# First attention and retention: scores and values in two stacked passes, first pair staged during the value rows

## The chip, the cores and the metric

The kernel runs on 1 core of one Trainium2 chip as one program written by hand for five engines: TensorE (matmuls), VectorE, ScalarE, GpSimd and SyncE, which issues the transfers. The metric is the device time of the core in microseconds (us). The engines meet through named counting semaphores: an instruction adds to one when it is done, another waits until the count is reached.

## The reference

Two transformer blocks on 512 tokens of width 1024, in float32. What matters here are two pieces, each with 8 heads of width 64:

```
# first block: stick-breaking attention
z = (q / 8) . k                                   # scores, per head
log_keep = where(s < t, log_sigmoid(-z), 0)
log_after = cumsum(log_keep, reversed) - log_keep
a = where(s < t, exp(log_sigmoid(z) + log_after), 0)
o = a . v
# second block: retention
scores = (rope(q) . rope(k)) * 64**-0.5 * gamma_h ** (t - s)   # for s <= t
o = scores . v                                     # then a group norm, times silu(gate)
```

log_sigmoid(-z) is minus softplus(z) = -log(1 + exp(z)), which is what the kernel calculates.

## The kernel before

**High and low parts.** Every float32 operand of a matmul is split into two parts of TensorE's faster type fp32r: ScalarE writes the high part (a copy that rounds), VectorE the low part (the full value less the high one). A product is then three passes into the same PSUM bank: high x high, high x low, low x high. Weights come in groups of 256 columns (1 MB) through two raw buffers: SyncE loads, ScalarE makes w_hi (1.9 us), VectorE w_lo (2.3 us), TensorE multiplies. A weight load waits until the low part of the group two before is made.

**The stages around the change.** In the first block the input is multiplied with the glu weights, then `qk` (4 groups, result qkT: four chunks of queries and four of keys, two heads of 64 rows in a chunk of 128 partitions), `val` (2 groups, value rows) and `gate` (8 groups). The gate matmuls are laid between the steps of the attention, one group to a head. In the second block the same is done with `ret_qk`, `ret_val` and then `latent` and `ret_gate` (2 groups each, one tile of 24 matmuls to a head). Meanwhile VectorE works through the taps of a convolution (`conv_beside`, `some_taps`; two taps of 0.75 us at a time) and columns of the modulation (`ada_column`).

**A pair of heads.** Before a pair starts, `stage_qk` on ScalarE and VectorE writes the parts of its queries (scaled by 1/8) and its keys. A chunk of keys holds both heads, so the queries of each head sit in a buffer of their own whose other 64 rows are zero (`clear_other_heads`, once for each stage): the contraction over 128 rows then gives one head. `stage_v` writes the high and low parts of the pair's values; the values product gives 128 rows of which the head's 64 are kept.

**A head of the attention** (`head` on TensorE L581, ScalarE L979, VectorE L1546):
1. TensorE: `scores`, four blocks of keys against the queries behind them (512, 384, 256 and 128 columns), three passes each, and a mask matmul. Into z, 1280 columns in two halves of 512 and 768.
2. VectorE: z clamped at 40 (L1554); ScalarE: exp, log(1 + x) (L985, L988); VectorE: the maximum with z (L1558); ScalarE and VectorE: high and low part (t_hi, t_lo). Beside it TensorE does 32 gate matmuls of 0.23 us each.
3. TensorE: running sums (L595, L598) from t_hi and t_lo into z; then 16 gate matmuls. Meanwhile ScalarE: exp of z, high part; VectorE: low part.
4. TensorE: `values` (L542), three passes; ScalarE moves the head's 64 rows of o_ps into qkT (L1006), behind a one-element write `apart`.

**A head of the retention**: scores; VectorE multiplies z with the decay (L1782), high and low part; TensorE has a tile of 24 matmuls beside it; values; ScalarE moves the result (L1222). From head 4 on pieces of the group norm and of the latent norm lie between (`beside_scores`, `beside_values`, `after_gate`); head 3 has the rotated key of the later attention (`key_rope`).

Each engine runs its list in order. `run` lays the step of one weight group (`ahead`) at a fixed place of each evacuation. The first pair is staged where one stage ends: on ScalarE behind the last value rows (L1008 to L1011; L1229 to L1236 in the retention), on VectorE behind the last modulation column (L1570, L1571; L1855 to L1857).

## Time and profile before

| | |
|---|---|
| median of 3 runs | 1462.67 us (1461.22 to 1462.8) |
| profiled execution: its time, its span | 1461.86 us, 1460.1 us |
| mean granted clock of TensorE | 0.979 |
| busy: TensorE, VectorE, ScalarE, GpSimd | 95%, 60%, 43%, 6% of the span |
| first attention with its gate groups | 143 to 292 us of the span |
| retention with latent and gate groups | 875 to 961 us |

A row of a timeline has the start, the duration, the engine, the line, the operation and what it writes and reads; in square brackets stands how long the engine was idle before it, and who released it. Rows of several instructions are merged (x8). TensorE overlaps a matmul with the next, so a row's duration is about 0.17 us longer than the distance to the next one's start. PEclk is the clock that TensorE was granted, as a share of 2.4 GHz.

### The profile page before, as it was taken

To read this page: it belongs to the slowest core of one execution; us is meant where nothing else is said; L and a number is where in the kernel's file an instruction comes from. 1 tells how busy PE (TensorE), PEld (TensorE's weight loads), DVE (VectorE), ACT (ScalarE), POOL (GpSimd) and SP (SyncE) were. 2 spreads that over 40 slices of the span, in tenths; PEclk is the share of its full clock that TensorE was granted. 3 is DMA by queue.
4 is the path that set the end of the run, shared out by engine and by line. 5 is a ranking of instruction groups with operands and counts; after the bars stand their busy time and mean duration, and the time that the engine had idled before them with its cause. 6 is when DMAs were issued, how large, how long until landed. Compare 5 with 4: busy or idle time off the path is not lost. (4 is left out here: it accounts for less than half of the span.)

```text
span 1460.1 us, 16589 instructions
## 1 busy us (share of the span) xinstructions
PE 1380.1 (95%) x6344; PEld 1134.4 (78%) x6344; DVE 872.8 (60%) x1057; ACT 629.3 (43%) x767; POOL 90.8 (6%) x67
## 2 busy tenths in 40 slices
PE   6998999979979999999997989988999999999997
PEld 3788888857748888888885788778778888888885
DVE  4799888768674432332335646777556754773663
ACT  4322666574354222221324744567645522432332
POOL 0000000010300093000001000000020000000001
PEclk9999999999989999999998999999999999999999
DMA  9532111035624423223231221040122232223212
GB/s 372 195 130 87 58 57 43 29 120 186 257 80 139 163 87 112 90 89 113 79 101 58 87 87 58 15 108 1 58 90 102 96 109 93 86 86 115 87 66 78
DMA packets 27110, 148.56 MB, mean 102 GB/s; under 512 B 3184, under 2 KB 3696, under 8 KB 14512
## 3 DMA queue, kind: packets, MB, share of 16 engines
q1 hardware_dynamic: 27056, 147.83, 28.2%
q8 instruction: 35, 0.57, 0.2%
q14 instruction: 19, 0.16, 0.0%
HBM read 143.88 MB, written 2.10 MB: 100 GB/s over the span
## 5 line engine op out<-in xcount | busy, mean ns | idle before, releaser
L1370 DVE TENSOR_TENSOR w_lo<-raw,w_hi 128x2048 fp32r<-128x2048 f32 (+2 forms) x114 | 251.5, 2206 | 122.4 <-ACT w_hi L838 118.9
L838 ACT ACTIVATE w_hi<-raw 128x2048 fp32r<-128x2048 f32 (+2 forms) x109 | 196.6, 1804 | 108.6 <-PE psum L482 80.6
L482 PE MATMUL psum<-h_hi,w_hi 128*128 128x512 f32 x712 | 180.0, 393 | 2.4 <-DVE w_lo L1370 2.4
L482 PE MATMUL psum<-h_hi,w_lo 128*128 128x512 f32 x712 | 178.0, 390 | 0.0
L482 PE MATMUL psum<-h_lo,w_hi 128*128 128x512 f32 x712 | 177.3, 389 | 0.0
L482 PEld LDWEIGHTS psum<-h_hi,w_hi 128*128 128x128 f32 x712 | 133.1, 189 | 31.0 <-DVE w_lo L1370 3.7
L482 PEld LDWEIGHTS psum<-h_lo,w_hi 128*128 128x128 f32 x712 | 133.6, 188 | 27.8
L482 PEld LDWEIGHTS psum<-h_hi,w_lo 128*128 128x128 f32 x712 | 133.1, 188 | 27.4
L482 PE MATMUL psum<-xg_hi,w_hi 128*128 128x512 f32 x336 | 83.0, 389 | 0.0
L482 PE MATMUL psum<-xg_hi,w_lo 128*128 128x512 f32 x336 | 83.0, 389 | 0.0
L482 PE MATMUL psum<-xg_lo,w_hi 128*128 128x512 f32 x336 | 83.0, 389 | 0.0
L1670 DVE TENSOR_TENSOR act_p<-act_a,psum 128x512 f32<-128x512 f32 x22 | 15.1, 688 | 112.3 <-PE psum L482 112.3
L482 PE MATMUL psum<-mid_hi,w_hi 128*128 128x512 f32 x312 | 77.7, 389 | 0.1
L482 PE MATMUL psum<-mid_hi,w_lo 128*128 128x512 f32 x312 | 77.6, 389 | 0.0
L482 PE MATMUL psum<-mid_lo,w_hi 128*128 128x512 f32 x312 | 77.5, 389 | 0.0
L482 PEld LDWEIGHTS psum<-xg_hi,w_lo 128*128 128x128 f32 x336 | 63.1, 188 | 13.1
L482 PEld LDWEIGHTS psum<-xg_hi,w_hi 128*128 128x128 f32 x336 | 63.1, 188 | 13.1
L482 PEld LDWEIGHTS psum<-xg_lo,w_hi 128*128 128x128 f32 x336 | 63.1, 188 | 13.1
L1968 DVE TENSOR_TENSOR up_raw<-psum,rs 128x512 f32<-128x512 f32 x44 | 30.3, 688 | 64.2 <-PE psum L482 59.6
L482 PEld LDWEIGHTS psum<-mid_hi,w_hi 128*128 128x128 f32 x312 | 58.5, 188 | 12.6 <-DVE w_lo L1370 0.5
L482 PEld LDWEIGHTS psum<-mid_hi,w_lo 128*128 128x128 f32 x312 | 58.6, 188 | 12.2
L482 PEld LDWEIGHTS psum<-mid_lo,w_hi 128*128 128x128 f32 x312 | 58.6, 188 | 12.2
(341 smaller groups left out, 2247.1 us busy)
## 6 DMA issues: line engine op xcount, KB each, us to landing
raw<-w_ffn_in SPq DMA_DIRECT2D x22, 1024.0 KB, 4.8
raw<-w_up SPq DMA_DIRECT2D x22, 1024.0 KB, 4.7
ada_first<-ada SPq DMA_DIRECT2D x16, 512.0 KB, 11.3
raw<-w_gate SPq DMA_DIRECT2D x8, 1024.0 KB, 4.7
raw<-w_mix_out SPq DMA_DIRECT2D x8, 1024.0 KB, 4.8
raw<-w_ffn_out SPq DMA_DIRECT2D x8, 1024.0 KB, 4.8
raw<-w_down SPq DMA_DIRECT2D x8, 1024.0 KB, 4.8
ada_mid<-ada SPq DMA_DIRECT2D x11, 512.0 KB, 6.0
```

The source lines that it names most:

```text
L482: last = mm(ps, w[slot][:, k, t * P:(t + 1) * P], part(xv, k0 + k), start=first, stop=final)
L838: A(w_hi[slot][:, 0:stage.kc, :], raw[slot][:, 0:stage.kc, :], ACT.Copy).then_inc(sem["w_hi_done"], 1)
L1370: return tt(out_lo, full, high.bitcast(F32), ALU.subtract)
L1670: free(stage, k, lambda: tt(act_p[s][:, :], act_a[s][:, :], bank[2 * s + 1], ALU.mult))
L1968: by_rs = lambda: tt(up_raw[t][s][:, :], bank[2 * s + t], rs[:, :], ALU.mult)
```

## The change

**Scores in two passes.** The zero rows of the query buffers get content: in `q_both` the head's own 64 rows hold the high part of its queries, the other 64 rows the low part. The keys then have to stand in both halves: `key_hi[s]` and `key_lo[s]` hold head s's keys twice. One pass with key_hi and one with key_lo give (high + low) x (high + low). **Values in two passes.** The weights for a head are 128 columns, 64 of high and 64 of low values (`att_v`, `ret_v`); the product gives 64 rows of each, which ScalarE copies (rows 0 to 63) and VectorE adds (rows 64 to 127, `add_low_part`, `join_head`). A product low x low is added that was not there before.

**Copies of the keys.** Transfers within SBUF bring the first head's keys into both halves of `key_dup` (2 x 512 KB) and, when they have landed, the second head's keys over the first's in qkT (512 KB). SyncE issues them in its list, before and between the loads of the first two groups of `gate` or `latent`. The same is done in the retention with rqk and `rkey_dup`.

**First pair.** `stage_qk(0)` moves to the second group of the value stage, on ScalarE in front of its evacuation and on VectorE behind the first group's modulation columns (in the retention behind the second group's weights, with two decays). The clears are gone. A pair's staging now has two full keys to split instead of one. `stage_v` moves on ScalarE to the end of the pair before.

**Softplus.** max(z, log(1 + exp(min(z, 40)))) becomes max(z, 0) + log(1 + exp(-|z|)): the clamp on VectorE goes, ScalarE takes the absolute value from PSUM, and the maximum and the addition are one VectorE instruction. The running sums of the first key block and the first block of the values now wait for the first half of t_lo alone.

The core of the difference (the declarations of buffers, the retention's twins of edits that are shown for the attention, and moved lines are left out):

```diff
@@ SyncE
+            def duplicate_first(keys, dup, done):
+                for s in range(2):
+                    sp.dma_start(dup[head_rows(s), :, :], keys[0:HD, PAIRS:, :]).then_inc(sem[done], 16)
+            def duplicate_second(keys, done):
+                sp.wait_ge(sem[done], 32)
+                sp.dma_start(keys[0:HD, PAIRS:, :], keys[HD:P, PAIRS:, :]).then_inc(sem[done], 16)
+            stage_loads(st["val"])
+            sp.wait_ge(sem["group_free"], st["val"].g0)
+            duplicate_first(qkT, key_dup, "key_dup")
+            load(st["gate"], 0, 0)
+            duplicate_second(qkT, "key_dup")
+            load(st["gate"], 1, 1)
...
+            sp.wait_ge(sem["rp_done"], 2 * PAIRS)
+            duplicate_first(rqk, rkey_dup, "rkey_dup")
+            load(st["latent"], 0, 0)
+            duplicate_second(rqk, "rkey_dup")
+            load(st["latent"], 1, 1)
@@ TensorE
-                    for n, (kk, qq) in enumerate(((key_hi, q_hi), (key_hi, q_lo), (key_lo, q_hi))):
-                        last = mm(z[:, a:a + w], kk[:, kb * P:(kb + 1) * P], qq[s][:, kb * P:S],
+                    for n, kk in enumerate((key_hi, key_lo)):
+                        last = mm(z[:, a:a + w], kk[s][:, kb * P:(kb + 1) * P], q_both[s][:, kb * P:S],
...
-                    for n, (vv, aa) in enumerate(((vs_hi, p_hi), (vs_hi, p_lo), (vs_lo, p_hi))):
-                        last = mm(o[:, kb * P:S], vv[:, v_at, kb * P:(kb + 1) * P], aa[:, a:a + w],
+                    if second and kb == 1:
+                        pe.wait_ge(sem[second[0]], second[1])
+                    for n, aa in enumerate((p_hi, p_lo)):
+                        last = mm(o[:, kb * P:S], v[:, s, kb, :], aa[:, a:a + w],
...
+                pe.wait_ge(sem["spl_done"], 2 * n + 1)
+                for part in (t_hi, t_lo):
+                    mm(z[:, 0:S], tri_r, part[:, 0:S], start=False, stop=True, skip_group_check=True)
                 pe.wait_ge(sem["spl_done"], 2 * n + 2)
...
-                pe.wait_ge(sem["al_done"], 2 * n + 2)
+                pe.wait_ge(sem["al_done"], 2 * n + 1)
+                values(o_ps, att_v, s, t_hi, t_lo, ("al_done", 2 * n + 2)).then_inc(sem["o_done"], 1)
@@ ScalarE
+            def stage_qk(i, q, dup):
+                for s in range(2):
+                    A(q_both[s][head_rows(s), :], chunk(q, i, head_rows(s)), ACT.Copy, scale=HD ** -0.5).then_inc(sem["qk_hi"], 1)
+                A(key_hi[0][:, :], chunk(dup, i), ACT.Copy).then_inc(sem["qk_hi"], 1)
+                A(key_hi[1][:, :], chunk(q, PAIRS + i), ACT.Copy).then_inc(sem["qk_hi"], 1)
+            def val_rows(i, s, k, ahead):
+                if k == 1:
+                    act.wait_ge(sem["key_dup"], 48)
+                    stage_qk(0, qkT, key_dup)
+                rows_of(st["val"], v_rows)(i, s, k, ahead)
...
+                for j, (a, b) in enumerate(HALVES):
+                    act.wait_ge(sem["z_done"], n + 1)
+                    A(zbuf[:, a:b], z[:, a:b], ACT.Abs).then_inc(sem["zm_done"], 1)
                 for j, (a, b) in enumerate(HALVES):
                     act.wait_ge(sem["zm_done"], 2 * n + j + 1)
-                    A(zbuf[:, a:b], zbuf[:, a:b], ACT.Exp).then_inc(sem["e_done"], 1)
+                    A(zbuf[:, a:b], zbuf[:, a:b], ACT.Exp, scale=-1.0).then_inc(sem["e_done"], 1)
...
-                apart(0)
-                A(chunk(qkT, i, rows), o_ps[rows, :], ACT.Copy).then_inc(sem["o_evac"], 1)
+                A(chunk(qkT, i, head_rows(s)), o_ps[0:HD, :], ACT.Copy).then_inc(sem["o_half"], 1)
+                if s and not final:
+                    stage_v(i + 1, v_rows, att_v)
@@ VectorE
-                for a, b in HALVES:
-                    ts(zbuf[:, a:b], z[:, a:b], 40.0, None, ALU.min).then_inc(sem["zm_done"], 1)
...
-                    tt(zbuf[:, a:b], z[:, a:b], zbuf[:, a:b], ALU.max).then_inc(sem["sp_done"], 1)
+                    stt(zbuf[:, a:b], z[:, a:b], 0.0, zbuf[:, a:b], ALU.max, ALU.add).then_inc(sem["sp_done"], 1)
...
                 some_taps(2, 3)
-            clear_other_heads()
-            stage_qk(0, 0, qkT, qkT)
+                dve.wait_ge(sem["o_half"], n + 1)
+                add_low_part(chunk(qkT, i, head_rows(s))).then_inc(sem["o_evac"], 1)
...
+            def join_head(n):
+                dve.wait_ge(sem["ro_half"], n + 1)
+                add_low_part(rqk[head_rows(n % 2), n // 2, :]).then_inc(sem["ro_evac"], 1)
```

What stood on ScalarE from the end of the first value group to the attention's first head; the `pair` buffers are the high parts of queries and keys, raw_52 and raw_53 the two weight buffers:

```order
L838 ACTIVATE w_hi_54<-raw_52 128x2048 [waits tile_done,raw_full0]
L961 ACTIVATE v_rows<-psum 128x2x256 [waits tile_done]
L963 ACTIVATE v_rows<-psum 128x2x256 [waits group_free,tile_done]
L1008 ACT_TABLE_LOAD
L973 ACTIVATE pair_78<-qkT 64x512 [waits ada_sum,group_free]
L973 ACTIVATE pair_79<-qkT 64x512
L974 ACTIVATE pair_82<-qkT 128x512
L861 UNCONDITIONAL_BRANCH
L861 ISA
L977 ACTIVATE att_v_hi<-v_rows 128x512
```

The same place in the changed kernel:

```order
L987 ACTIVATE v_rows<-psum 128x2x256 [waits group_free,tile_done]
L993 ACTIVATE pair_77<-qkT 64x512 [waits key_dup]
L993 ACTIVATE pair_78<-qkT 64x512
L994 ACTIVATE pair_79<-key_dup 128x512
L995 ACTIVATE pair_80<-qkT 128x512
L862 ACTIVATE w_hi_54<-raw_52 128x2048 [waits tile_done,raw_full0]
L985 ACTIVATE v_rows<-psum 128x2x256 [waits tile_done]
L987 ACTIVATE v_rows<-psum 128x2x256 [waits group_free,tile_done]
L998 ACTIVATE att_v<-v_rows 128x4x2x64 [waits ada_sum,group_free]
```

The staging of queries and keys, now four instructions with a wait for the copies, has moved ahead of the gate weights and of the second group's value rows; behind the rows only the values remain.

VectorE at the end of an odd head with a next pair, before; qkT is where a head's output goes, conv_77 and conv_tmp are the taps' sums:

```order
L1501 SCALAR_TENSOR_TENSOR conv_tmp<-u,vec,conv_tmp 128x512
L1500 REGISTER_ALU
L1501 ISA [waits tap]
L1501 SCALAR_TENSOR_TENSOR conv_77<-u,vec,conv_77 128x512
L1399 REGISTER_ALU
L1399 COMPARE_AND_BRANCH
L1370 TENSOR_TENSOR att_v_lo<-v_rows,att_v_hi 128x512 [waits v_hi]
L1554 TENSOR_SCALAR zbuf<-psum 128x512 [waits z_done]
L1554 TENSOR_SCALAR zbuf<-psum 128x768
L1501 SCALAR_TENSOR_TENSOR conv_tmp<-u,vec,conv_tmp 128x512 [waits tap]
L1501 SCALAR_TENSOR_TENSOR conv_77<-u,vec,conv_77 128x512 [waits tap]
L1558 TENSOR_TENSOR zbuf<-psum,zbuf 128x512 [waits l_done]
```

The same place in the change (conv_76 is the sum that was conv_77):

```order
L1556 SCALAR_TENSOR_TENSOR conv_76<-u,vec,conv_76 128x512
L1604 REGISTER_ALU
L1538 ISA [waits o_half]
L1538 TENSOR_TENSOR qkT<-psum,qkT 64x512
L1435 REGISTER_ALU
L1435 COMPARE_AND_BRANCH
L1406 TENSOR_TENSOR att_v<-v_rows,att_v 128x4x2x64 [waits v_hi]
L1556 SCALAR_TENSOR_TENSOR conv_tmp<-u,vec,conv_tmp 128x512 [waits tap]
L1556 SCALAR_TENSOR_TENSOR conv_76<-u,vec,conv_76 128x512 [waits tap]
L1593 SCALAR_TENSOR_TENSOR zbuf<-psum,zbuf 128x512 [waits l_done]
L1593 SCALAR_TENSOR_TENSOR zbuf<-psum,zbuf 128x768 [waits l_done]
L1406 TENSOR_TENSOR t_lo<-zbuf,t_hi 128x512 [waits sph_done]
```

A wait for ScalarE's copy and the join stand between the last tap and the next pair's values, and the two clamps are gone.

SyncE between the loads of the value weights and the loop over the gate groups, in the change (before, the loop over all gate groups followed at once):

```order
L326 DMA raw_52<-w_val 128x2048 [waits w_lo_done]
L326 DMA raw_53<-w_val 128x2048 [waits w_lo_done]
L330 REGISTER_ALU
L330 COMPARE_AND_BRANCH
L378 DMA key_dup<-qkT 64x2048 [waits group_free]
L378 DMA key_dup<-qkT 64x2048
L326 DMA raw_52<-w_gate 128x2048 [waits w_lo_done]
L383 DMA qkT<-qkT 64x2048 [waits key_dup]
L326 DMA raw_53<-w_gate 128x2048 [waits w_lo_done]
```

The three copies stand in the list with their waits, so the first two gate groups are loaded behind and between them.

## Rows read from the trace of the kernel before

**Rows 1.** Timeline of TensorE at the attention's first scores: start us, us, engine, line, operation, idle before.

```profile
143.07 1.62 PE L531 MATMUL psum<-pair,pair 128*128 128x512 f32 x3 [5.18 <-DVE pair L1370]
...
147.48 2.62 PE L482 MATMUL psum<-h_hi,w_hi 128*128 128x512 f32 x8
```

**Rows 2.** Timeline of TensorE at the retention's first two heads.

```profile
875.04 3.76 PE L531 MATMUL psum<-pair,pair 128*128 128x512 f32 x12 [5.23 <-DVE pair L1370]
...
878.59 2.35 PE L482 MATMUL psum<-h_hi,w_hi 128*128 128x512 f32 x8
...
886.27 2.08 PE L531 MATMUL psum<-pair,pair 128*128 128x512 f32 x12
...
888.19 2.04 PE L482 MATMUL psum<-h_hi,w_hi 128*128 128x512 f32 x8
```

**Rows 3.** Busy us (x instructions) by stretch: PE, PEld, DVE, ACT, POOL, PEclk, DMA share, GB/s.

```profile
140.00:145.00 5.00, 1.93 (x5) 1.68 (x6) 4.22 (x8) 2.25 (x4) 0.00 (x0) 0.69 0.01 3
...
870.00:880.00 10.00, 4.96 (x17) 4.48 (x18) 3.16 (x6) 6.82 (x11) 0.00 (x0) 0.66 0.00 0
...
964.00:970.00 6.00, 4.15 (x17) 2.69 (x15) 4.45 (x7) 3.10 (x6) 0.00 (x0) 1.00 0.99 203
```

**Rows 4.** Timeline of TensorE, end of head 1 to the gate matmuls of head 3.

```profile
178.24 1.97 PE L482 MATMUL psum<-h_lo,w_hi 128*128 128x512 f32 x8
...
180.40 0.50 PE L542 MATMUL psum<-t_hi,att_v_hi 128*128 128x512 f32 x1 [0.19 <-DVE t_lo L1370]
...
182.38 0.90 PE L531 MATMUL psum<-pair,pair 128*128 128x512 f32 x3
...
184.75 2.06 PE L482 MATMUL psum<-h_hi,w_hi 128*128 128x512 f32 x8
...
203.00 2.06 PE L482 MATMUL psum<-h_hi,w_hi 128*128 128x512 f32 x8
```

**Rows 5.** Timeline of TensorE, retention heads 4, 6 and the queries behind them.

```profile
922.73 1.95 PE L654 MATMUL psum<-rope_t,ones 128*128 128x512 f32 x4 [1.03 <-ACT rope_t L1174]
...
948.02 1.10 PE L646 MATMUL psum<-rope_t,block_mean 128*128 128x512 f32 x2 [1.02 <-ACT rope_t L1161]
...
968.49 1.10 PE L646 MATMUL psum<-sq_up,block_mean 128*128 128x512 f32 x2 [1.85 <-ACT sq_up L1161]
```

**Rows 6.** Timeline of VectorE before the attention's first head.

```profile
138.27 0.08 DVE L1442 DVE_READ_ACCUMULATOR2_ANT mod<- 128x1 f32 x1
...
140.87 1.34 DVE L1537 SCALAR_TENSOR_TENSOR pair<-qkT,pair 64x512 fp32r<-64x512 f32 x2
```

**Rows 7.** Timelines of ScalarE and VectorE, attention head 1.

```profile
168.84 1.35 ACT L988 ACTIVATE zbuf<-zbuf 128x512 f32<-128x512 f32 x2
...
175.71 0.63 ACT L974 ACTIVATE pair<-qkT 128x512 fp32r x1
...
176.55 1.30 ACT L998 ACTIVATE zbuf<-psum 128x512 f32<-128x512 f32 x2 [0.21 <-PE psum L595]
...
166.50 1.55 DVE L1554 TENSOR_SCALAR zbuf<-psum 128x512 f32<-128x512 f32 x2 [2.01 <-PE psum L534]
...
172.10 0.96 DVE L1370 TENSOR_TENSOR t_lo<-zbuf,t_hi 128x768 fp32r<-128x768 f32 x1 [0.32 <-ACT t_hi L991]
...
178.19 0.69 DVE L1370 TENSOR_TENSOR pair<-qkT,pair 128x512 fp32r<-128x512 f32 x1
```

**Rows 8.** Timeline of VectorE, retention head 3 to 4.

```profile
914.32 0.69 DVE L1751 TENSOR_TENSOR rope_t<-psum,sin_mla 64x512 f32<-64x512 f32 x1
...
916.48 1.68 DVE L1782 TENSOR_TENSOR rp<-psum,decay 128x512 f32<-128x512 f32 x4
```

**Rows 9.** Timelines of VectorE and TensorE at the attention's end.

```profile
292.08 0.75 DVE L1501 SCALAR_TENSOR_TENSOR conv<-u,vec,conv 128x512 f32<-128x512 f32 x1
...
293.34 1.96 PE L616 MATMUL psum<-u,ones 128*128 128x512 f32 x4 [0.99 <-ACT qkT L1006]
```

**Rows 10.** Timeline of VectorE, last rotated key of the retention.

```profile
850.69 0.69 DVE L1737 TENSOR_TENSOR rqk<-rope_t,swapped 128x512 f32<-128x512 f32 x1
```

More of the change, by code:

```diff
@@ L325, in load, with stage_loads @@
                              dram["w_" + stage.name][bass.ds(k, 1)].rearrange("g p n -> p (g n)")).then_inc(raw_full[slot], 16)
-            def stage_loads(stage):
-                with sp.Fori(0, stage.n // 2) as i:
+            def stage_loads(stage, begin=0):
+                with sp.Fori(begin, stage.n // 2) as i:
                     for s in range(2):
@@ L372, in _ @@
                 load(st["qk"], k, k - 2)
[L373 to L374 removed]
+            def duplicate_first(keys, dup, done):
[10 more added lines that the diff above has]
+            load(st["gate"], 1, 1)
+            stage_loads(st["gate"], 1)
+            stage_loads(st["att_out"])
             sp.wait_ge(sem["o_evac"], HEADS)
@@ L594, in head @@
                     for part in (t_hi, t_lo):
-                        last = mm(z[:, a:a + w], tri_r, part[:, a:a + w], start=False, stop=True, skip_group_check=True)
+                        if kb:
+                            last = mm(z[:, a:a + w], tri_r, part[:, a:a + w], start=False, stop=True, skip_group_check=True)
                         for later in range(kb + 1, QB):
@@ L993, in head @@
                 A(chunk(gates, 2 * n), bank[2 * s], ACT.Copy)
-                if not ahead() and s:
-                    stage_qk(i + 1, qkT, qkT)
+                final = ahead()
+                if s and not final:
+                    stage_qk(i + 1, qkT, key_dup)
                 for j, (a, b) in enumerate(HALVES):
@@ L1122, in _, with decays @@
             run(st["ret_qk"], rotary)
+            def decays(n):
+                A(decay[n % 4][:, :], lag[:, :], ACT.Exp, scale=scol("log_gamma", n)).then_inc(sem["dec_done"], 1)
             def values_by_rs(i, s, k, ahead):
                 ahead()
+                if k == 1:
+                    act.wait_ge(sem["rkey_dup"], 48)
+                    stage_qk(0, rqk, rkey_dup)
+                    act.wait_ge(sem["in_lag"], 16)
+                    for n in range(2):
+                        decays(n)
                 if k == 0:
@@ L1483, in _, with stage_qk, stage_v, add_low_part @@
                 free(st["glu"], k, lambda: tt(u[:, k, PAD:PAD + S], glu_sig[k % 2][:, :], bank[2 * k], ALU.mult))
+            def stage_qk(i, staged, q, dup):
+                for s in range(2):
+                    dve.wait_ge(sem["qk_hi"], 4 * staged + 4 * i + s + 1)
+                    stt(q_both[s][head_rows(1 - s), :], chunk(q, i, head_rows(s)), HD ** -0.5, q_both[s][head_rows(s), :].bitcast(F32),
+                        ALU.mult, ALU.subtract).then_inc(sem["qk_lo"], 1)
+                for s, full in enumerate((chunk(dup, i), chunk(q, PAIRS + i))):
+                    dve.wait_ge(sem["qk_hi"], 4 * staged + 4 * i + 3 + s)
+                    less(key_lo[s][:, :], full, key_hi[s][:, :]).then_inc(sem["qk_lo"], 1)
+            def stage_v(i, staged, v, both):
+                dve.wait_ge(sem["v_hi"], staged + i + 1)
+                part_of = lambda k: both[:, :, :, HD * k:HD * k + HD].rearrange("p s b d -> p b s d")
+                less(part_of(1), v[:, :, bass.ds(P * i, P)].rearrange("p b (s d) -> p b s d", s=2), part_of(0)).then_inc(sem["v_lo"], 1)
+            def add_low_part(dst):
+                return tt(dst, o_ps[HD:P, :], dst, ALU.add)
             sums = [conv_tmp, conv3]
@@ L1518, in evac @@
                             ada_column(val_bufs[r], ADA_FIRST + r)
+                        if step == 4:
+                            stage_qk(0, 0, qkT, key_dup)
                 return evac
```

119 lines of the change are left out of this document (46 added, 73 removed).

## The prediction

> **What bounds the kernel now.** I read the page first: TensorE is busy 95% of the span (the table above), so a change pays where it removes work from TensorE or a wait in front of it. Then I read TensorE's timeline over the two stages that the change touches: the first attention (143 to 292 us) and the retention (875 to 961 us). The reader is to see three things. First, both stages begin with a hole: TensorE idles 5.18 us [rows 1] and 5.23 us [rows 2] until VectorE has written the low parts of the first pair, and both are followed by matmuls at the lower clock (mean granted clock 0.69 and 0.66, [rows 3]). Secondly, inside the stages TensorE goes from matmul to matmul: one head of the attention lasts 18.25 us (184.75 to 203.00) or 18.45 us [rows 4], one of the early retention heads 9.28 us, and its idle time there is a few tenths before each values product. Thirdly, from head 4 of the retention on there are waits on ScalarE of about 1 us [rows 5]. So passes taken from TensorE are worth their full time, up to the point where the chains on ScalarE and VectorE end last.
>
> **Passes removed.** Scores and values each drop one of three passes over four blocks of 512, 384, 256 and 128 columns. In the attention the twelve values matmuls run from 180.40 to 182.38, 1.98 us [rows 4]; scores with four mask matmuls take 2.37 us (182.38 to 184.75), of which the masks are some 0.3. In the retention scores take 1.92 us (886.27 to 888.19, [rows 2]). A third of 1.92 is 0.64; I take 0.63 for each pass. 8 heads x 2 passes x 0.63 = 10.1 us in each stage, 20.2 us together. Bounds: 0.57, if all 1280 columns went at the pace of a gate tile's row (8 matmuls of 512 columns in the 1.81 us between such rows), and 0.69, a third of the scores' 2.07 us without masks: 18 to 22 us.
>
> The Trainium skill, "TensorE: Matmul & The Clock Gate", section "Back-to-back issue gap", gives the isolated gap of a matmul at full clock as N/2.4 + 2.5 ns. By that a pass of 1280 columns would be worth 0.54 us and the term 17.4 us. By that rule, the trace does not agree to the tenth: its pass is 0.64 us in the retention's scores.
>
> **First boundary (137.8 us).** Before, TensorE waits 5.2 us, runs the scores in 4.41 us (143.07 to 147.48, [rows 1]) where another head takes 2.37 [rows 4], so 2.04 us more, and the first gate pass in 2.62 where the same row elsewhere reads about 2.0: 0.6 more. That is 7.8 us. Now the staging stands among the value rows. The key copies can be issued when the last query-key tile is evacuated, at 115.5 us. Nearest row for their speed: copies within SBUF move 203 GB/s with the DMA engines 99% busy [rows 3]. 1.05 MB then takes 5.2 us, and with about 1.7 us from issue to first bytes (256 KB landed alone in 3.0 us, less 1.3 us of data) it lands at about 122.5; the gate weights behind it at about 126; the second copy (0.52 MB, 2.6 us) at about 128.5. ScalarE comes to it at 127.0, behind the first group's value rows, and stages until 131; VectorE adds two pieces of 0.67 us and two of 0.69, 2.8 us, and ends its list at 141.1 instead of 138.3 [rows 6]. The four clears and its old staging are gone. TensorE can begin its scores at 137.8 without a wait; margin about 4 us. What is late next is VectorE: conv start, the low values part and two taps bring it to 144.0, while the logarithm of head 0 would be ready at 142.9. The running sums then wait about 0.4 us. Gain 7.4 us.
>
> The Trainium skill, "DMA: Bandwidth & Descriptors", section "Anatomy of one DMA", gives 2.0 us plus bytes at 436 GB/s: the first copies would land in 4.4 us, not 6.9. The rows of this kernel's copies within SBUF show less than half that speed; by the page the margins below would only be wider, the sum the same, and late copies less likely.
>
> **Inside an attention head.** The clamp on VectorE (1.55 us) becomes an absolute value on ScalarE. Nearest row: two halves read from PSUM, 1.30 us; exponentials and logarithms follow at 1.26 to 1.35 us a pair [rows 7]. Scores' end to logarithm: 2.37 us before (166.47 to 168.84), forecast 0.04 + 1.18 + 1.26 = 2.5 us. Bounds: -0.3 us (the clamp's way saved) and +1.5 us (nothing overlaps). VectorE's max-and-add may cost 0.1 us more a head. Low parts were ready at 173.06 [rows 7], TensorE came at 173.63: slack 0.57, and now the first two matmuls (0.45 us) need only the first half. The sums start as before; cost nothing. If that cover went, each further 0.1 us a head would cost 0.8 us in all.
>
> Before the values, even heads wait 0.17 us and odd ones 0.35 (its last gate row starts at 178.24 and needs 1.81; values at 180.40, [rows 4]). With only the first half needed for the first block, the even ones (and head 7) wait no more: -0.17 x 5 = -0.85. Heads 1, 3 and 5 also stage the next pair, and that has grown by one full key: 0.63 us on ScalarE, 0.69 on VectorE [rows 7]. ScalarE's key ended at 176.34, 0.2 us before the sums; now 0.7 us after the exponentials could start. VectorE reaches the low part 0.8 us later, TensorE waits about 0.3 and, at the second block, 0.4: 0.7 for 0.35. +0.35 x 3 = +1.05. Together +0.2 us. The join (64x512 from PSUM, 0.69 us by [rows 8]) waits on VectorE for ScalarE's copy of the upper half; queued behind it are the next low values part and two taps, which end about C + 9.0 us (C the end of the running sums) while the next logarithm comes at C + 9.65: hidden by 0.6 us, by 0.25 in odd heads. At the stage's end it isn't hidden: VectorE has taps until 292.8 [rows 9], then the join, so the mean's first matmul comes 7.0 us after the sums' end where it was 6.76 (293.34). That forfeits head 7's 0.63 + 0.17 and 0.24 more: +1.0 us.
>
> Attention: -10.1 - 7.4 + 0.2 + 1.0 = -16.3 us.
>
> **Retention boundary (869.7 us).** Wait 5.23, scores 3.55 us (875.04 to 878.59) for 1.92, first tile pass 2.35 for 2.04 [rows 2]: 5.2 + 1.6 + 0.3 = 7.1 us. The copies start when the last key is rotated, 851.4 [rows 10]: landed 858.6, latent weights 862 (they were loaded from 842.7; SyncE's order now holds them back 10 us), second copy about 865. ScalarE splits the weights 862 to 864 (before at 859), stages 865 to 867.6, computes two decays, then evacuates; VectorE's last low key is ready at about 868.9. TensorE arrives at 869.65: margin 0.8 us, the thinnest of the change. Gain 7.1, between -0.3 and 7.2 if the copies come up to 8 us later.
>
> **Inside the retention.** Heads 0 to 3: scores' end to low part is about 4.7 us, TensorE's tile 5.5 us, the join lies beside ScalarE's copy of 1.27 us. All passes count. Head 3 to 4: VectorE has the rotated key besides and came to head 4 at 916.48 [rows 8], already 0.1 us late. Now it has 0.69 us more (second key) and the scores end 1.3 us earlier; the squares of head 4 move with VectorE, so the wait at 922.73 [rows 5] grows: values 3 and scores 4 are not gained (1.26) and 0.6 is lost: +1.9. Head 5: ScalarE's further key delays its squares: +0.6. Head 6: ScalarE is the chain from the output of head 5 to 948.02, so scores 6 are not gained: +0.6. Behind head 7 the join, the first query and ScalarE's table load stand in line up to 968.49 [rows 5]; of the last three passes (1.9 us) about 1.1 arrives: +0.8.
>
> Retention: -10.1 - 7.1 + 1.9 + 0.6 + 0.6 + 0.8 = -13.3 us.
>
> **Sum.** The profiled execution took 1461.86 us (span 1460.1), 0.8 below the median of 1462.67, within what the runs differ. 1461.86 - 16.3 - 13.3 = 1432.3. I add 0.7 us for the thin margin at the retention's copies (one chance in ten of 7 us): 1433.0 us.
>
> **Rivals.**
> The chains bind. If ScalarE's three functions in a row, or the join, do not overlap as I read them (upper bound +1.5 us between scores and logarithm), TensorE waits some 0.6 us more in each of 16 heads: +10, 1443 us. For it: slacks of 0.25 to 0.8 us. Against it: every duration is from rows of the same shapes.
> The copies are late. Landing 6 us later costs the retention's whole boundary and about 1 us at the attention's: +8, 1441 us. For it: three transfers in one queue and the weights between them. Against it: the mk copies' measured speed.
> A pass is worth only its columns: the matmul that goes is then one whose weight load and hand-over lay beside others. At the low bound from rows, 0.57, 32 x 0.06 = 1.9 us are missing: 1434.9 us. This is the mechanism behind the Trainium skill's gap above.
> The change doesn't do what it says: the first pair is staged no earlier and the third passes were hidden. 1462 us. Nothing speaks for it, since TensorE has no idle time that would take up the passes.
> Slower: waits before the values grow so long that the clock falls behind each of them, as it did at both boundaries, where it cost 2.6 us (2.04 + 0.6) at 143 us. 16 x (0.7 + 2.6) = 53 us: 1486 us. It decides from the point where 11 of the 16 heads fall (29 / 2.6). Against it: a wait of 1.85 us before 968.49 left the granted clock at 1.00 [rows 3, 5], and the forecast waits are 0.7 us at most in the attention.
>
> **How the numbers follow.** Forecast 0.72 (own range 1428 to 1438), chains 0.10, copies 0.10, the smaller pass 0.05, slower 0.02, nothing 0.01. A measurement of this kernel tells about 0.2% (3 us) from no change. Faster 0.97, same 0.01, slower 0.02. The range runs from 1427.5 (all passes at 0.69 us, -1.9, and 3.6 of the 5.1 us of new waits absent) to 1443, where the chains or late copies would put it.
>
> **What would show each step.** TensorE's wait before the first scores of each stage: under 0.5 us and no lower clock at 140 or 872 us. A head of the attention: 16.9 us (even) and 17.6 us (odd with staging); a retention head 8.0 us up to head 3. Before head 4's squares a wait of near 3 us. The mean's matmul 7.0 us after the sums. If an attention head takes over 18 us, or scores two thirds of which were kept take over 1.9 us, I am wrong on the chain or the pass; if TensorE stands at 870 us for VectorE's low key, the copies were late.

## The result, and the profile after

| | before | after |
|---|---|---|
| median of 4 runs each, us | 1461.95 (1460.01 to 1462.8) | 1444.09 (1442.05 to 1445.13) |
| profiled span, us | 1460.1 | 1443.1 |
| mean granted clock | 0.979 | 0.977 |

Ratio 0.9874, 95% interval 0.9862 to 0.9887: 18.4 us faster (16.5 to 20.2). The forecast was 1433.0 us, in 1427.5 to 1443: the direction held, 11 of the 29 us did not come, and the time lies 1.1 us outside the range.

To find where, take an instruction that both kernels have and subtract its start after from its start before: that is the gain up to there. The first group of rows is TensorE's timeline of the changed kernel through the attention (start us, duration us, engine, line, operation, idle before it and who ended it).

```profile
137.10 0.63 PE L555 MATMUL psum<-pair,pair 128*128 128x512 f32 x2
...
146.85 0.50 PE L618 MATMUL psum<-t_hi,rounded 128*128 128x512 f32 x1 [0.57 <-DVE t_lo L1406]
...
155.40 0.67 PE L555 MATMUL psum<-pair,pair 128*128 128x512 f32 x2
...
172.82 0.68 PE L555 MATMUL psum<-pair,pair 128*128 128x512 f32 x2
...
174.56 2.06 PE L506 MATMUL psum<-h_hi,w_hi 128*128 128x512 f32 x8
...
189.53 0.67 PE L555 MATMUL psum<-pair,pair 128*128 128x512 f32 x2
...
276.79 2.59 PE L645 MATMUL psum<-u,ones 128*128 128x512 f32 x4 [2.19 <-DVE qkT L1538]
```

The wait of 5.18 us ahead of the first scores [rows 1] is gone. Heads take 17.42 us (155.40 to 172.82) and 16.71 (to 189.53) where they took 18.45 and 18.25 [rows 4]; scores with masks take 1.74 us (172.82 to 174.56) for 2.37. The mean's first matmul starts at 276.79, before at 293.34 [rows 9]: gain 16.55 us, forecast 16.3.

Behind it the gain shrinks. The same timeline of the changed kernel, then of the kernel before, at the statistics of the convolution's norm:

```profile
281.60 0.80 PE L519 MATMUL psum<-h_hi,w_hi 128*128 128x512 f32 x1
...
295.92 2.07 PE L467 MATMUL psum<-sq_sum,ones 128*128 128x512 f32 x2 [2.85 <-POOL sq_sum L2060]
297.01 2.69 PE L506 MATMUL psum<-h_hi,w_hi 128*128 128x512 f32 x4
...
302.45 0.84 PE L506 MATMUL psum<-h_hi,w_hi 128*128 128x512 f32 x3
```

```profile
296.45 0.80 PE L495 MATMUL psum<-h_hi,w_hi 128*128 128x512 f32 x1
...
310.79 1.13 PE L443 MATMUL psum<-sq_sum,ones 128*128 128x512 f32 x2 [2.87 <-POOL sq_sum L2015]
311.35 1.50 PE L482 MATMUL psum<-h_hi,w_hi 128*128 128x512 f32 x4
...
314.52 1.07 PE L482 MATMUL psum<-h_hi,w_hi 128*128 128x512 f32 x4
```

The eight matmuls of the mean took 3.11 us before (293.34 to 296.45) and now 4.81 (276.79 to 281.60): gain 14.85. The statistics wait as long as before (2.85 us for 2.87), yet what follows is slower: gain 12.07 at 302.45. Gain 10.9 at the end of retention's value rows (869.65 before, 858.74 after): of the 1.2 us lost on the way, 0.7 stands in TensorE's wait for ScalarE before the next norm's sums of squares (6.71 us for 6.00), 0.3 behind the wait of 3.94 us before the convolution's second stage, which low clock followed before the change too.

The retention in the changed kernel, on TensorE:

```profile
861.07 2.08 PE L555 MATMUL psum<-pair,pair 128*128 128x512 f32 x8 [2.16 <-issue]
862.94 3.05 PE L506 MATMUL psum<-h_hi,w_hi 128*128 128x512 f32 x8
...
870.68 1.43 PE L555 MATMUL psum<-pair,pair 128*128 128x512 f32 x8
871.95 2.06 PE L506 MATMUL psum<-h_hi,w_hi 128*128 128x512 f32 x8
...
879.63 1.46 PE L555 MATMUL psum<-pair,pair 128*128 128x512 f32 x8 [0.79 <-DVE pair L1406]
...
896.61 1.46 PE L555 MATMUL psum<-pair,pair 128*128 128x512 f32 x8 [0.79 <-DVE pair L1406]
...
905.62 3.35 PE L683 MATMUL psum<-rope_t,ones 128*128 128x512 f32 x4 [2.04 <-ACT rope_t L1214]
...
951.00 2.05 PE L675 MATMUL psum<-sq_up,block_mean 128*128 128x512 f32 x2 [2.65 <-ACT sq_up L1201]
```

Against [rows 2]: 2.16 us of the 5.23 are left, with slow matmuls behind. Two new waits of 0.79 us stand ahead of the scores of heads 2 and 4; measured by starts a head with such a wait takes 8.97 us instead of 8.00, so each costs 0.97. Head 4's statistics (`rope_t` x ones, the sums of squares for the latent's norm) wait 2.04 us for 1.03 [rows 5], the last variance 2.65 for 1.85 [rows 5], and the instructions themselves take 3.35 us for 1.95 and 2.05 for 1.10.

Busy time by stretch for those four places, the kernel before ahead of the changed one (columns as in [rows 3]; PEclk is the granted clock):

```profile
293.00:297.00 4.00, 3.66 (x9) 1.77 (x10) 2.50 (x4) 2.39 (x5) 0.00 (x0) 1.00 0.00 0
308.00:315.00 7.00, 4.21 (x17) 3.13 (x18) 3.11 (x3) 5.42 (x6) 2.53 (x2) 1.00 0.86 332
922.00:928.00 6.00, 5.27 (x22) 3.61 (x23) 4.40 (x6) 1.66 (x4) 0.00 (x0) 1.00 0.27 87
968.00:973.00 5.00, 4.51 (x16) 3.10 (x17) 3.57 (x6) 3.33 (x6) 0.00 (x0) 1.00 0.96 238
```

```profile
276.00:282.00 6.00, 5.21 (x9) 2.21 (x10) 3.14 (x5) 2.19 (x4) 0.00 (x0) 0.72 0.00 0
295.00:302.00 7.00, 6.08 (x13) 4.14 (x14) 1.95 (x1) 3.56 (x4) 0.87 (x1) 0.51 0.64 239
905.00:911.00 6.00, 5.38 (x12) 2.76 (x13) 2.99 (x4) 1.00 (x2) 0.00 (x0) 0.72 0.30 90
950.00:955.00 5.00, 4.00 (x8) 2.10 (x9) 2.85 (x5) 3.40 (x6) 0.00 (x0) 0.66 0.97 247
```

Four places that ran at full clock before do not now; behind the attention's first scores the low clock of [rows 3] is gone (1.00 from 137 to 142 us). The mean over the run barely moved, so it hides this.

Why the first scores of retention are late stands on the timelines of the DMA queue, ScalarE and VectorE in the changed kernel:

```profile
840.50 1.13 SPq L378 DMA_DIRECT2D rkey_dup<-rqk  x2
841.68 2.03 SPq L326 DMA_DIRECT2D raw<-w_latent  x1
847.50 0.46 SPq L383 DMA_DIRECT2D rqk<-rqk  x1
848.00 0.58 SPq L326 DMA_DIRECT2D raw<-w_latent  x1
...
853.97 1.92 ACT L862 ACTIVATE w_hi<-raw 128x2048 fp32r<-128x2048 f32 x1 [5.70 <-DMA raw<-w_latent]
857.34 1.28 ACT L993 ACTIVATE pair<-rqk 64x512 fp32r<-64x512 f32 x2 [1.45 <-DMA rqk<-rqk]
...
855.91 2.29 DVE L1406 TENSOR_TENSOR w_lo<-raw,w_hi 128x2048 fp32r<-128x2048 f32 x1 [12.64 <-ACT w_hi L862]
858.24 1.41 DVE L1525 SCALAR_TENSOR_TENSOR pair<-rqk,pair 64x512 fp32r<-64x512 f32 x2
...
860.28 0.68 DVE L1406 TENSOR_TENSOR pair<-rqk,pair 128x512 fp32r<-128x512 f32 x1
```

Two transfers that the staging needs are late. The first latent weights (1 MB, issued at 841.68) land at 853.96, the second copy (512 KB, issued at 847.50) at 857.33, 9.8 us after its issue; half a microsecond behind it another 1 MB of weights was put into the same queue. TensorE was there at 858.91. What it waits for is VectorE's last low key, ready at 860.96, and VectorE works without a gap from 855.91 on: the low part of the first latent weights, then the staging. So the weights' landing sets the wait. The second copy follows closely: ScalarE has the second key's high part at 859.8, so without the late weights VectorE's last low key would come at about 860.5 (an estimate: 859.8 and the 0.7 us of its row), half a microsecond earlier.

Theory from here: the passes and the early staging gave what was forecast, and the missing 11 us are (a) transfers sharing the queue at retention's start, (b) VectorE's staging ending behind the values, (c) lower clock behind short waits. Rival: the passes are worth less than 0.63 us since the chains bind.

### The profile page after: what moved, and what is told of

It is laid out like the page before. It is cut to its first block and busy times, and to the rows that moved or that the text cites. A ratio compares the mean times of both kernels' runs of the same rounds, so it can differ in the third digit from the quotient of the medians.

```text
span 1443.1 us, 16364 instructions
## 1 busy us (share of the span) xinstructions
PE 1364.2 (95%) x6216; PEld 1115.5 (77%) x6216; DVE 872.9 (60%) x1057; ACT 638.8 (44%) x782; POOL 90.5 (6%) x67
## 5 line engine op out<-in xcount | busy, mean ns | idle before, releaser
L1705 DVE TENSOR_TENSOR act_p<-act_a,psum 128x512 f32<-128x512 f32 x22 | 15.1, 687 | 112.4 <-PE psum L506 112.4
L506 PEld LDWEIGHTS psum<-mid_hi,w_hi 128*128 128x128 f32 x312 | 58.5, 188 | 12.6 <-DVE w_lo L1406 0.5
```

Of the source, the lines that this page charges most:

```text
L506: last = mm(ps, w[slot][:, k, t * P:(t + 1) * P], part(xv, k0 + k), start=first, stop=final)
L1705: free(stage, k, lambda: tt(act_p[s][:, :], act_a[s][:, :], bank[2 * s + 1], ALU.mult))
```

## The experiments

Each stands against runs of the kernel before on the same chip (medians 1461.9 to 1462.8).

**Third pass put back.**

```
-for n, kk in enumerate((key_hi, key_lo)):
+for n, kk in enumerate((key_hi, key_lo, key_lo)):
-for n, aa in enumerate((p_hi, p_lo)):
+for n, aa in enumerate((p_hi, p_lo, p_lo)):
```

> The changed kernel with one more pass in the scores and in the values of every head of both stages (the low part is multiplied twice, so the numbers differ in the last digits; it stands for the third pass of before). Theory: a pass is worth 0.63 us on the path in each of 16 heads, 32 of them 20.2 us; in retention they fill the two waits of 0.79 us at the pair boundaries (-1.6), so 1444.1 + 18.6 = about 1463, heads of the attention 17.4/18.1 us. Rival one, the chains over ScalarE and VectorE bind in the heads and the missing 11 us were never in the passes: under +12 us, 1456 or less. Rival two, a pass is worth only its columns at 0.445 ns (0.57): +16.6, 1461.

Measured 1456.69 us, ratio 0.9966 [0.9952, 0.9979]: +12.6. The theory's 18.6 missed; the total fits the first rival. Its rows don't:

```profile
158.38 0.91 PE L555 MATMUL psum<-pair,pair 128*128 128x512 f32 x3
...
194.82 0.91 PE L555 MATMUL psum<-pair,pair 128*128 128x512 f32 x3
...
879.69 2.08 PE L555 MATMUL psum<-pair,pair 128*128 128x512 f32 x12
...
889.29 2.11 PE L555 MATMUL psum<-pair,pair 128*128 128x512 f32 x12 [0.16 <-DVE pair L1406]
...
917.22 1.95 PE L683 MATMUL psum<-rope_t,ones 128*128 128x512 f32 x4 [1.41 <-ACT rope_t L1214]
```

Two heads of the attention take 36.44 us (158.38 to 194.82) for 34.13: 0.58 us a pass. Scores of retention grow by 0.65 us. But the waits of 0.79 shrink to 0.16, 2.04 to 1.41, 2.65 to 1.84, and the statistics run in 1.95 us, at full clock. From the first scores of retention to the last variance the kernel is 4.7 us longer (94.6 for 89.9) where eight heads have 10.1 us of matmuls more. So the passes are worth their size while they stand in a row, and the chains at the ends of stages, with the clock, take back over a third (7.6 of 20.2). My expectation had counted only two of those waits.

**Late staging.**

```
-act.wait_ge(sem["key_dup"], 48); stage_qk(0, qkT, key_dup)     # in val_rows
+act.wait_ge(sem["key_dup"], 48); stage_qk(0, qkT, key_dup)     # ahead of run(gate)
... the same on VectorE, and both for rqk behind ret_val
```

> The changed kernel with the staging of the first pair of both stages behind the value rows again, everything else kept. Theory: the attention's boundary is worth what its rows gave (7.4) and retention's only about 3 to 4, since its second copy came late and the clock fell there: +10 to +12 us, 1455. Rival, both boundaries are worth their forecast and the loss lies all elsewhere: +14.5, 1458.6. Rival, early staging hinders later work: +8 or less, 1452.

Measured 1452.30 us, 0.9938 [0.992, 0.9957]: +8.2, below the theory, at the second rival. By rows the second head of the attention starts 6.2 us later (161.60 for 155.40) and retention loses 2.6 more. But the low clock behind the convolution's statistics is absent here (their two matmuls take 1.13 us, not 2.07), which gives 2.8 us back; without that the edit would cost 11.0, in the theory's range, so the second rival isn't shown.

**Fillers.** Matmuls into a bank that nobody reads, at four waits.

```
+fill(bank[4], h_hi[:, 0, :], 8)    # ahead of the mean
+fill(bank[4], h_hi[:, 4, :], 10)   # ahead of stat_sum("conv_ln")
+fill(o_ps, h_hi[:, 0, :], 7)       # ahead of head 4's statistics
+fill(bank[4], lat_hi[:, 0, :], 9)  # ahead of group_var(.., 2, ..)
```

> The changed kernel with matmuls that nobody reads put into four waits of TensorE: 8 of 128x512 before the mean (wait 2.19), 10 before the statistics of the convolution's norm (2.85), 7 before head 4's squares (2.04), 9 before the variance beside the up-projections (2.65). They add work and take no wait's end away. Theory (the clock falls behind these waits, and that is where some of the missing time went): no granted clock under 1.00 behind those places, the matmuls behind them at full rate, -1.7 -2.5 -1.7 -1.0 = -6.9 us, 1437 (1436 to 1440 where a filler ends late). Rival (the low clock costs nothing since other engines end last, or the clock falls at the next wait instead): 1443 to 1446.

Measured 1442.86 us, 0.9875 [0.9854, 0.9896]: 1.2 us less than the changed kernel, within what medians differ, so the time does not decide. Its stretches do:

```profile
279.00:284.00 5.00, 4.71 (x14) 2.34 (x13) 3.01 (x6) 2.84 (x6) 0.00 (x0) 1.00 0.00 0
296.00:303.00 7.00, 6.38 (x27) 4.62 (x26) 2.84 (x2) 3.73 (x4) 1.07 (x1) 1.00 0.71 261
903.00:909.00 6.00, 5.64 (x25) 3.74 (x24) 4.55 (x6) 2.34 (x5) 0.00 (x0) 1.00 0.27 87
947.00:952.00 5.00, 4.61 (x17) 3.17 (x18) 3.56 (x7) 3.21 (x6) 0.00 (x0) 1.00 0.93 256
```

At all four the clock stays at 1.00, with waits of 0.29 to 0.62 us left. From the mean to the first matmul of the mix (`mix_out`, the stage that joins the outputs) it takes 58.77 us for 63.34 (-4.6, forecast -4.2), from retention's first scores to the last variance 88.07 for 89.93 (-1.9), and behind the variance 1.4 less. Two things took 5.7 of these 7.8 us back: the last attention (+2.9; the granted clock was 0.74 from 1008 to 1021 us, where the changed kernel had 0.86 from 1011 to 1023, so the rival's "at the next wait" is right in part), and a first head that waited 2.21 us for VectorE where the profiled run of the changed kernel waited 0.57. The second copy of keys was late again:

```profile
133.20 1.28 ACT L1002 ACTIVATE pair<-qkT 64x512 fp32r<-64x512 f32 x2 [5.83 <-DMA qkT<-qkT]
...
149.69 0.50 PE L623 MATMUL psum<-t_hi,rounded 128*128 128x512 f32 x1 [2.21 <-DVE t_lo L1415]
```

ScalarE stages at 133.20 instead of 129.21, VectorE's columns and taps queue behind, TensorE waits inside head 0, and the mean starts 2.9 us later. The same stands in the third-pass run (1.95 us). So the attention's copies were at the edge too, which one trace had hidden.

**Staging by head.** Query and key of head 0, then of head 1, on ScalarE and VectorE (not shown) and in TensorE's wait.

```
-                if s == 0:
-                    pe.wait_ge(sem["qk_lo"], 4 * i + 4)
+                pe.wait_ge(sem["qk_lo"], 4 * i + 2 * s + 2)
```

> The changed kernel with a pair staged head by head (query and key of head 0, then of head 1) on ScalarE and VectorE, and the scores of a head waiting for its own half alone; the first head of a stage so waits for the first two copies of keys only. Theory (VectorE's 2.7 us of staging ends 0.8 us behind the values): the waits of 0.79 us before the scores of heads 2 and 4 of retention go, and the wait of 2.16 us at its start falls to 0.9 or less with its low clock: -1.6 -1.3 to -2.8 = -2.9 to -4.4, 1440 to 1441. Rival (these waits are cover for the chain behind them, which then waits as much in the head's values): 1443 to 1444.

Measured 1441.87 us, 0.9861 [0.9836, 0.9885]: -2.2, a little short, and the interval overlaps the changed kernel's, so the rows have to decide. Heads 1 to 4 of retention start 8.00 us apart (871.62, 879.62, 887.62, 895.62), the forecast's 8.0, so the waits of 0.79 us (0.97 by starts) were VectorE's staging. But head 4's statistics then wait 3.13 us for 2.04, which takes 1.1 of 1.9 back: the rival is right in that part. In the attention the edit costs: the mean starts at 279.57 for 276.79. That the time fell even so is clock, 1.00 here behind the mean and behind head 4's statistics (1.7 us each), which the edit does not explain.

Retention's first wait stayed (2.06), although head 0 no longer needs the second copy. VectorE shows why:

```profile
858.20 2.29 DVE L1405 TENSOR_TENSOR w_lo<-raw,w_hi 128x2048 fp32r<-128x2048 f32 x1 [13.86 <-ACT w_hi L860]
...
861.24 0.69 DVE L1405 TENSOR_TENSOR pair<-rkey_dup,pair 128x512 fp32r<-128x512 f32 x1
```

Head 0's two low parts again stand directly behind the low part of the first latent weights, whose load landed at 856.2, and TensorE starts at 862.03. This run takes the second copy out of the wait and leaves the wait: the late weights are enough for it.

**Loads apart.**

```
+load(st["latent"], 0, 0)
 sp.wait_ge(sem["rp_done"], 2 * PAIRS)
 duplicate_first(rqk, rkey_dup, "rkey_dup")
-load(st["latent"], 0, 0)
 duplicate_second(rqk, "rkey_dup")
+sp.wait_ge(sem["rkey_dup"], 48)
 load(st["latent"], 1, 1)
... the same for qkT, key_dup and the gate's weights
```

> The changed kernel with the 1 MB weight load that stood between the key copies issued ahead of them and the next one held until the second copy has landed, in both stages. Theory (the second copy shares the queue with that load: 9.8 us for 0.5 MB in retention, 7.3 to 10.3 in the attention): it lands in 4.5 to 5.5 us, the wait of 2.16 us at retention's start and the low clock behind it go, -3.5; in the attention the staging on ScalarE comes before 129 in every run and the first head's wait stays at 0.6, -0 to -1.5: 1439.5 to 1441. Rival (the boundary in retention is set by the high parts of the weights and the value rows' copies, not by the key copies): wait of 1.5 us or more stays, 1443 to 1444.

Measured 1435.61 us, 0.9812 [0.9799, 0.9825]: -8.5, twice what was expected, with nothing but the order and the waits of SyncE's transfers changed.

```profile
834.81 1.13 SPq L378 DMA_DIRECT2D rkey_dup<-rqk  x2
841.66 0.46 SPq L383 DMA_DIRECT2D rqk<-rqk  x1
845.76 0.34 SPq L326 DMA_DIRECT2D raw<-w_latent  x1
...
853.05 1.39 PE L557 MATMUL psum<-pair,pair 128*128 128x512 f32 x8
854.27 2.06 PE L508 MATMUL psum<-h_hi,w_hi 128*128 128x512 f32 x8
856.17 1.98 PE L508 MATMUL psum<-h_hi,w_lo 128*128 128x512 f32 x8
```

The second copy lands 4.1 us after its issue (9.8 before the edit). The first latent weights, issued at 826.13, are there long before ScalarE takes them at 842.46, and VectorE's last low key is ready at 849.5. TensorE's first scores of retention wait for nothing, and the tiles behind them run at full rate. The edit does two things, the load ahead of the copies and the next one held back, and no run separates them. From the value rows' end to the second tile pass the gain over the kernel before grows by 8.0 us (16.6 to 24.6), 7.4 without the head's own pass: forecast 7.1. The stretches behind the mean and behind the convolution's statistics are at 1.00 as well, although their waits are unchanged (2.19 and 2.85 us): 3.2 us of the gain up to the mix (3.9 us) is clock that this edit does not explain, and 1.8 us more come between the mix and the end of retention's value rows, where nothing was edited.

**Squares first.**

```
+if n == 4:
+    latent_squares()
 act.wait_ge(sem["rp_f"], n + 1)
```

> The changed kernel with ScalarE's two squares of the latent done before head 4's high part instead of behind it, the weights' high part and a copy. Theory: the wait of 2.04 us before head 4's statistics goes and the low clock behind it, -2.0 -1.4 = -3.4 us, 1440.7; what stays is the wait for the head's low part, some 0.3. Rival (the head's own chain over rp and its parts ends as late): 1443.5.

Measured 1445.88 us, 0.9879 [0.9864, 0.9894]: no gain. Up to the third square's sum 3.0 us were gained (19.52 us from head 4's scores for 22.56) and 2.7 lost behind it; and the first head waited 2.23 us for the late copy.

**Mean and statistics moved.**

```
-pe.wait_ge(sem["o_evac"], HEADS); mm(o_ps, ones, ...)
+mm(bank[4], ones, ...)
-stat_sum("conv_ln")              # ahead of weight group 2
+... stat_sum("conv_ln")          # behind it
```

> The changed kernel with two edits at the end of the attention: the mean's matmuls go into bank 4 and so no longer wait for the last head's output to be joined, and the sum of the convolution's squares stands one weight group (5.4 us) later. Theory: the waits of 2.19 and 2.85 us and the low clock behind both go or fall under 1 us: -1.3 -1.7 and -2.8 -2.5, less 1 for what comes late behind = -7, 1437. Rival (the chain over POOL, ScalarE and VectorE to the convolution's second stage sets the end, so that the wait of 3.94 us before it grows by as much): 1441 to 1444.

Measured 1438.77 us, 0.9838 [0.9824, 0.9851]: -5.3. The mean waits 1.37 us, now for VectorE's taps; the wait at the statistics is gone, and from the mean to the mix's first matmul it takes 56.88 us for 63.34. The wait ahead of the convolution's second stage grew from 3.94 to 5.18.

**Up-projections first.**

```
-up_query(2); up_query(3); ...; group_var(bank[0], 2, sq_up)
+up_query(2) ... up_query(6);   group_var(bank[0], 2, sq_up)
```

> The changed kernel with three more up-projections (4.1 us) ahead of the group variance that waited 2.65 us for ScalarE's square. Theory: wait and low clock go, -2.6 -1.4 = -4.0, of which the chain over VectorE to the first scores of the last attention (wait 2.12 us now) takes back about half: 1442. Rival one: all is taken back, 1444 to 1445. Rival two: all is kept, 1440.

Measured 1442.38 us, 0.9865 [0.985, 0.9881]: -1.7, the expected 1442, though the runs of the two kernels overlap. By rows the edit is worth 2.6 us: the wait of 2.65 us is 0.32, and from the first up-projection to the last attention's scores it takes 20.28 us for 22.88.

**Loads apart with the third pass.** The first and the fifth edit together.

> The kernel with the loads apart (1435.6) and the third pass of before put back in scores and values, as in the first experiment. There the pass cost 12.6 us net: the rows gave 0.6 us a pass in each head, less waits and low clock that the longer heads covered and a first head that began 2.3 us later. Theory: with the copies apart the same count holds, 20.2 less about 5 us of covered waits and low clock in retention and 1.3 behind the attention = +14, 1449.5. Rival (the first experiment's 12.6 held two effects of the copies that cancelled; without them the passes are worth their full 20.2): 1455.5. Rival: less than 12, 1447 or under.

Measured 1449.51 us, 0.992 [0.9907, 0.9934]: +13.9 over the loads apart, the theory's number. The rival that the copies had hidden the passes' full 20.2 us falls.

**Combinations.** Loads apart, staging by head in retention, the mean and statistics, the up-projections; then with the squares first, or with two fillers (7 ahead of head 4's statistics, 16 ahead of the convolution's second stage).

> All that gained at once: loads apart (-8.5), the pairs of retention staged by head (-1.6 of waits), the mean in bank 4 and the convolution's statistics one weight group later (-5.3, of which some 1.5 was low clock that the loads alone also spared), the up-projections ahead of the variance (-1.7). Theory (they stand in different places and add): 1444.1 - 8.5 - 1.6 - 3.8 - 1.7 = 1428.5. Rival (each gain shifts the others' clock and half is given back): 1432 or more.

Measured 1431.51 us, 0.9799 [0.9786, 0.9812]: 3 us short. The loads apart had already spared the clock behind the mean and the statistics: from the mean to the mix the combined kernel takes 57.55 us for their 60.10, 2.5 less where 3.8 were added up. And head 4's statistics now wait 3.14 us.

> The combined kernel with ScalarE's latent squares before head 4's high part as well. Alone that edit gained 3.0 us up to head 5 and gave 2.7 back by the end (wait before the third square's sum 1.94 instead of 1.02, and later ones). Theory: again within 1 us of the combined kernel, 1427.5 to 1429.5. Rival (what gave it back was the up-projections' wait, which is gone now): 3 us less, 1425.5.

Measured 1428.15 us, 0.9772 [0.9759, 0.9785]: 3.4 us less, the rival's size, but the rows don't bear the rival out. Between the two profiled executions (spans 1428.0 and 1424.7 us) 2.3 of the 3.3 us stand ahead of retention's first scores (853.31 and 850.99), where both kernels are the same; from there on the squares are worth 1.0. Head 4's wait is gone, and the next one, before the third square's sum, is 2.47 us with low clock behind.

> The combined kernel with fillers at two waits that remain: 7 matmuls of 128x512 before head 4's statistics (wait 2.04) and 16 before the convolution's second stage (wait 5.2 with the statistics later; 3.6 us of work). Theory (the clock falls behind both): -1.7 behind head 4 and -1.5 to -2 behind the second, 1425 from 1428.5. Rival (the clock falls at the next wait instead or other engines end last): within 1 us of the combined kernel.

Measured 1426.76 us, 0.9757 [0.9741, 0.9773]: 4.8 us less than the combined kernel, with no overlap of their runs, and the fastest of all, 17 us under the changed kernel. The rows give the fillers less than that. From the mean to the mix it takes 55.98 us for 57.55 (-1.6, granted clock 1.00 for 0.62 from 307 to 315 us). From the mix to retention's first scores, where nothing differs, it takes 516.6 for 519.0 (-2.4), and from there to the end 1.2 more. So kernels with work that nobody needs can be faster, and how much of the 4.8 us that work is worth stays open.

## Why the prediction was wrong

- **Passes.** 0.63 us each held in the scores: 2.37 to 1.74 and 1.92 to 1.27 us. Put back, a pass cost 0.58 us in the attention's heads, near the low bound (0.57), and 0.65 in retention's scores. The chains inside the attention's heads did not bind. In all the prediction counted 20.2 us less 5.1 of waits, 15.1; with the loads apart the third pass costs 13.9.
- **First boundary and heads of the attention.** Right: no wait, heads 17.4 and 16.7 us for 17.6 and 16.9, gain 16.55 for 16.3. The margin of "about 4 us" at the copies was not there: ScalarE waited 2.83 us for the second copy and VectorE's last low key was ready at 134.7, 2.4 us before TensorE came, and in five of the other kernels with that order of loads the first head waited 1.95 to 2.25 us.
- **Retention boundary, the step that failed first:** "latent weights 862 ... second copy about 865". I let each transfer run alone behind the one ahead of it, the second copy in 2.6 us. In the queue three of them were under way at once: the second copy was issued while the weights' load was in flight, and the next load 0.5 us behind the copy. Counted from the last rotated key the first latent weights landed 13.5 us later instead of 10.6, the second copy 16.8 instead of 13.6. VectorE's low part of those weights and the staging behind it ended as much later, which turned a margin of 0.8 us into a wait of 2.16 with low clock: 3.4 of 7.1 us gained. With the loads apart it is 7.4. The weights' load ended last and the second copy half a microsecond before it; the run staged by head, which doesn't need that copy for its first scores, waited as long. The rival "the copies are late" named the queue ("the weights between them"), but with a chance of 0.10; the order of the queue was in the code, and the thinnest margin deserved more. The fit cited there from the Trainium skill, "DMA: Bandwidth & Descriptors", is one for transfers that GpSimd issues, and SyncE issues these; no term of the sum rested on it.
- **Retention, heads 0 to 3:** "All passes count" failed by 2 x 0.97 us. The prediction holds the head's low part and the join against TensorE's tile, and says nothing of VectorE's staging of the next pair, for which the next scores wait.
- **Head 4:** the wait is 2.04 us, forecast near 3. Where the two waits ahead of it were taken away it read 3.13, so the step was right and the unforecast waits had made TensorE late. The clock then fell as well.
- **Clock:** forecast at nothing, from a single row at 1.00 behind 1.85 us [rows 5]. Four places fell, at the ends of stages and not in the heads where the "slower" rival looked: from the wait to the first row at full rate 1.7 us behind the mean (4.81 for 3.11 us), 2.8 behind the statistics, 1.7 behind head 4's wait and 1.4 behind the last variance's, 7.6 us. Held at full clock, TensorE took 4.6 and 1.9 us less over the stretches from the mean to the mix and through the retention.
- **The sum:** between the profiled executions 29.6 us were forecast and 17.0 came. Clock 7.6, the boundary 3.7, the staging waits 1.9, 1.2 on the way to retention and 0.3 in heads 5 to 7 make 14.7. Against it stand 0.9 us of waits up to head 4's statistics that were forecast and did not come, 0.3 more gained in the attention and 0.9 behind the last variance, which leaves the 12.6. This is a count of rows, not a proof of each. With the copies apart the same kernel takes 1435.6 us, 2.6 from the forecast, of which some 5 us (3.2 and 1.8 above) is time in places that the edit doesn't touch: luck.

## What to carry to other kernels

A transfer that is waited for shares its queue with all that is under way in it: price them together, issue early what the chain needs first, and hold the next load until it has landed. Then follow the chain back from the instruction that waits; the late transfer that the eye falls on need not be the one that ends last, and another can stand close behind it. Removing matmuls shifts TensorE against chains at the ends of stages that it used to cover: list each wait it arrives at earlier, and hold a staging step against the first instruction that reads it. Where a wait of 2 us or more remains, price lower clock behind it, and move useful matmuls into it. And where a small edit is judged by the whole time, compare the stretches too: here 2 us of some differences stood where nothing was edited.

## What was unexpected

- The same wait is followed by low clock in one kernel and not in another. Behind the mean's wait of 2.19 us the first four matmuls took 2.59 us in the changed kernel, 3.65 with the squares first, 1.96 staged by head and with the loads apart. Behind the statistics' 2.85 us their two took 2.07, 1.12, 2.07 and 1.13 (in the second, the squares first, the fall came just behind them: 0.67 over 4 us); ahead of head 4's sums a wait of 3.13 us left 1.96 where 2.04 us gave 3.35. What decides between them is open, and a forecast can only give it a chance. A count over the profiled executions of all fourteen kernels, at these four places and retention's start, gives one: behind waits of 2.0 to 3.2 us the granted clock of the next 4 us was under 1.00 in 24 of 35 cases, behind waits of 0.3 to 1.9 us in none of 22.
- The Trainium skill, "TensorE: Matmul & The Clock Gate", section "What's actually happening", says that the gate follows how busy TensorE has been. The fillers agree (four stretches of 0.51 to 0.72 went to 1.00), with the reserve that some of these places were at 1.00 without them in other kernels; the equal waits above show that a wait's length alone does not say it.
- 512 KB copied within SBUF landed in 4.1 us alone and in 9.8 us between two loads of 1 MB, one still in flight and one issued 0.5 us behind it. Which of the two slowed it no run separates.
- The same code between the mix and retention's first scores took 516.6 to 519.0 us in the three combined kernels.
